# GLU chunk behind four gate chunks, S5 steps one per chunk, parameter rows on the sync queue, masks built late

## The reference

```
h      = rms_norm(x)
proj   = h @ w_in                 # q,k,v (512 each), u (256), q_mem (256), 3 x 1024 gate logits
o_na   = neighbourhood_attention(q, k, v, bias table)      # 8 heads, clamped 8 x 16 windows
o_s5   = GLU(gelu(bidirectional S5 state space layer(u)))   # 16 groups x 16 channels, 64 complex states
o_xa   = cross_attention(q_mem, rms_norm(mem) @ w_mem_kv)   # 4 heads, 256 memory tokens
merged = sum over the 3 branches of sigmoid(gate logits + b_gate) * (o_branch @ w_branch)
x      = x + merged @ w_out
x      = x + MoE(rms_norm(x))     # 16 experts of width 256 in 4 groups, top 2 in the best group
return rms_norm(x) * final_norm
```

## Time and profile before

| | us |
|---|---|
| median of 3 runs | 766.08 (764.28 to 766.26) |
| the profiled execution, its own time | 761.52 |
| its span | 759.9 |
| TensorE busy with matmuls | 648.5 (85%) |
| VectorE, ScalarE, GpSimd busy | 428.0, 325.2, 177.7 |
| mean granted TensorE clock | 0.933 of full |

### The profile page before, as it was taken

How to read it: one execution, slowest core, us unless ns; L and a number is a source line. 1 busy time by engine, 2 the same in 40 slices (tenths; PEclk the granted TensorE clock), 3 DMA queues, 4 the chain that set the end, 5 groups by cost and what they waited for, 6 DMA issues and landing times.

```text
span 759.9 us, 9239 instructions
## 1 busy us (share of the span) xinstructions
PE 648.5 (85%) x3201; PEld 512.7 (67%) x3201; DVE 428.0 (56%) x784; ACT 325.2 (43%) x549; POOL 177.7 (23%) x188
## 2 busy tenths in 40 slices
PE   1889899799799999999999997998378999989820
PEld 1667778697577776677777785887356777777610
DVE  5987016905623454334552259442667998999803
ACT  3872322203244333344322337222256787768612
POOL 7519819500000000000000000001363352324220
PEclk9999899989799999999999999998589999999965
DMA  9963112214121112411122224416968999999455
GB/s 287 183 157 104 36 40 72 84 56 111 30 81 56 56 56 76 146 57 56 55 70 70 83 84 136 146 56 244 351 199 294 324 383 363 354 345 319 114 80 225
DMA packets 88625, 114.73 MB, mean 151 GB/s; under 512 B 18336, under 2 KB 65538, under 8 KB 88584
## 3 DMA queue, kind: packets, MB, share of 16 engines
q1 hardware_dynamic: 74288, 92.56, 36.8%
q0 software_dynamic: 6848, 18.36, 10.0%
q10 hardware_dynamic: 7448, 3.27, 1.5%
HBM read 102.08 MB, written 15.80 MB: 155 GB/s over the span
## 4 chain that ended last, share of the span: by engine, by line
PE 55%; DMA 19%; DVE 11%; issue 6%; ACT 5%; POOL 2%; ACTq 1%; DVEq 0%; POOLq 0%; SPq 0%
DMA acc_scratch<-ysb,idx 17%; PE bank L1391 13%; PE bank L1393 12%; PE bank L1392 12%; PE bank L1571 3%; PE bank L1543 2%; PE bank L1560 2%; DVE w_lo L897 2%; PE bank L1547 1%; PE bank L1505 1%; PE bank L1481 1%; ACT w_hi L513 1%; POOL tok_scratch L1950 1%; DVE h_lo L922 1%; PE bank L1473 1%
## 5 line engine op out<-in xcount | busy, mean ns | idle before, releaser
L897 DVE TENSOR_TENSOR w_lo<-raw,w_hi 128x1024 fp32r<-128x1024 f32 x55 | 69.5, 1265 | 155.0 <-ACT w_hi L513 154.6
L1391 PE MATMUL bank<-h_hi,w_hi 128*128 128x512 f32 x320 | 131.8, 412 | 3.8 <-DVE w_lo L897 1.9
L1393 PE MATMUL bank<-h_hi,w_lo 128*128 128x512 f32 x320 | 125.3, 392 | 0.0
L1392 PE MATMUL bank<-h_lo,w_hi 128*128 128x512 f32 x320 | 125.0, 390 | 0.0
L1312 DVE TENSOR_TENSOR e_lo<-eraw,e_hi 128x2048 fp32r<-128x2048 f32 x48 | 108.5, 2286 | 12.8 <-ACT e_hi L796 12.8
L796 ACT CAST e_hi<-eraw 128x2048 fp32r<-128x2048 f32 x48 | 91.8, 1916 | 5.8 <-PE bank L1393 5.8
L1922 POOL DMA_DIRECT2D h_scratch<-h x4 | 2.2, 555 | 378.9 <-DVE h L1243 378.9
L1391 PEld LDWEIGHTS bank<-h_hi,w_hi 128*128 128x128 f32 x320 | 60.2, 188 | 18.6 <-DVE w_lo L897 2.6
L513 ACT CAST w_hi<-raw 128x1024 fp32r<-128x1024 f32 x55 | 57.4, 1044 | 34.5 <-PE bank L1393 34.5
L1393 PEld LDWEIGHTS bank<-h_hi,w_lo 128*128 128x128 f32 x320 | 60.0, 188 | 13.4
L1392 PEld LDWEIGHTS bank<-h_lo,w_hi 128*128 128x128 f32 x320 | 60.3, 189 | 10.5
(11 more groups left out here) (372 smaller groups left out, 1325.7 us busy)
## 6 DMA issues: line engine op xcount, KB each, us to landing
raw<-in_w_in SPq DMA_DIRECT2D x40, 512.0 KB, 3.8
eraw<-in_moe_w_gate SPq DMA_DIRECT2D x32, 512.0 KB, 7.3
eraw<-in_moe_w_up SPq DMA_DIRECT2D x32, 512.0 KB, 11.5
eraw<-in_moe_w_down SPq DMA_DIRECT2D x32, 512.0 KB, 9.4
raw<-in_w_out SPq DMA_DIRECT2D x8, 512.0 KB, 3.8
x_sb<-in_x SPq DMA_DIRECT2D x4, 512.0 KB, 5.2
raw<-in_w_mem_kv SPq DMA_DIRECT2D x4, 512.0 KB, 7.8
x_sb<-in_x SPq DMA_DIRECT2D x1, 2048.0 KB, 10.8
```

Source lines behind the costliest of these rows:

```text
L897: dve.tensor_tensor(v(l_, o, [1, 1024]), v(raw, 1024 * (c % RAW), [1, 1024]), raw32(v(h_, o, [1, 1024])), SUB).then_inc(sem("w_lo_done"), 1)
L1391: pe.matmul(dst, w[0], x[0], start=first, stop=False)
L1392: pe.matmul(dst, w[0], x[1], start=False, stop=False)
L1393: return pe.matmul(dst, w[1], x[0], start=False, stop=last)
```

## The change

- `C_GLU` goes from 20 to 24: four S5 gate chunks (20 to 23) now stand ahead of the GLU chunk, and the other four behind it. For that, `gt` lies in the room of x (42.5 KB) and no longer shares room with the split y, and the first gate's take has no wait for the GLU. The slots keep their places relative to the gate chunks. The first gate chunk waits until y has been taken out of banks 2 and 3.
- `s5_matrices` is cut in pieces: `turn_b` behind chunks 8 and 9 (16 transposes each, banks 4, 5, 7, 3), `lags` behind 10, `shifts` behind 11. `s5_inputs` goes from behind chunk 9 to behind 12. VectorE's steps go from 9 to 14 to 12 to 17, `s5_outputs` from behind 15 to behind 18, `gelu_arg` and `gelu` from steps 18 and 19 to 21 and 22. The rotations share one small buffer `turned_z`. The wait for the second turned memory value goes from the transposes to `shifts`.
- The bias flips are cut in two, two behind chunk 4 and two behind chunk 5, with ScalarE's copies.
- The eight parameter transfers go from ScalarE's queue to SyncE's, between the loads of chunks 0 and 1. The 16 transfers that bring y back go from ScalarE's to SyncE's, behind the load of chunk 25, with the wait for y in DRAM. The second load of x goes from between chunks 40 and 41 to behind all loads and the wait for the last product, ahead of the first expert weights.
- The ten mask instructions go on GpSimd from its start to behind the matrices `ca`.

The core of the diff:

```diff
-C_U, C_QX, C_MEMK, C_MEMV, C_Q, C_K, C_V, C_GLU = 0, 2, 4, 6, 8, 12, 16, 20
-C_S5G, C_S5P, C_XAG, C_XAP, C_NAG, C_NAP, C_OUT = 21, 29, 31, 39, 41, 49, 53
+C_U, C_QX, C_MEMK, C_MEMV, C_Q, C_K, C_V = 0, 2, 4, 6, 8, 12, 16
+C_S5G, C_GLU, C_S5P, C_XAG, C_XAP, C_NAG, C_NAP, C_OUT = 20, 24, 29, 31, 39, 41, 49, 53
...
-    gt = at("gt", R0 + 16, KD * SEQ)
+    gt = at("gt", 42.5, KD * SEQ)
...
         load(0)
+
+        def rows(w, r, n):
+            sp.dma_start(v(prm, 0, [1, P], p0=r, pn=n), w).then_inc(sem("prm_in"), 16)
...
-        for c in range(5, C_NAG):
+        for c in range(5, NCH):
             load(c)
-
-        sp.wait_ge(sem("s5_y"), 2)
-        sp.dma_start(v(x_sb, 0, [D, NT], [1, D]), x_nat).then_inc(sem("x_again"), 16)
-        for c in range(C_NAG, NCH):
-            load(c)
+            if c == 25:
+                sp.wait_ge(sem("y_out"), 16)
+                for g in range(G5):
+                    sp.dma_start(v(yT, SEQ * (g // 8), [K5, T5], [1, K5], p0=16 * (g % 8), pn=16),
+                                 y_dram.rearrange("(t c) (g k) -> c t g k", c=16, k=K5)[:, :, g, :]).then_inc(
+                                     sem("y_in"), 16)
...
         sp.wait_ge(sem("prod"), 24)
+        sp.dma_start(v(x_sb, 0, [D, NT], [1, D]), x_nat).then_inc(sem("x_again"), 16)
         load_unit(0, 0, 0)
...
-                elif m == 0:
-                    act.wait_ge(sem("s5_lo"), 2)
...
-            if c == 8:
-                take_s5_matrices()
-            if c == 15:
+            if c in (8, 9):
+                take_b(4 * (c - 8))
+            if c == 10:
+                take_lags()
+            if c == 11:
+                take_shifts()
+            if c == 18:
                 take_y()
-            if c == 16:
-                load_y()
-            if c == 18:
+            if c == 22:
                 act.wait_ge(sem("gelu_in"), 1)
...
-            if c in (9, 11):
-                rotate_in((c - 9) // 2)
-            if c in (10, 12):
-                scans((c - 10) // 2)
-            if c in (13, 14):
-                rotate_out(c - 13)
-            if c == 18:
+            if c in (12, 14):
+                rotate_in((c - 12) // 2)
+            if c in (13, 15):
+                scans((c - 13) // 2)
+            if c in (16, 17):
+                rotate_out(c - 16)
+            if c == 21:
                 gelu_arg()
-            if c == 19:
+            if c == 22:
                 gelu()
...
             if c == C_S5G:
+                pe.wait_ge(sem("y_took"), 1)
+            if c == C_S5G + 2:
                 pe.wait_ge(sem("v_took"), 6)
...
-            if c == 8:
-                pe.wait_ge(sem("bias_ready"), 4)
-                s5_matrices()
-            if c == 9:
+            if c in (8, 9):
+                turn_b(4 * (c - 8))
+            if c == 10:
+                lags()
+            if c == 11:
+                shifts()
+            if c == 12:
                 s5_inputs()
-            if c == 15:
+            if c == 18:
                 s5_outputs()
```

More of the change, by code:

```diff
@@ L66, in tiles_of @@
         return [("k", c - C_K)]
[L67 removed]
+    if c < C_S5G:
         return [("v", c - C_V)]
@@ L73, in tiles_of @@
             turns = TURNS.get(c, ())
-            return [(name + "t", j) for j in turns] + [(name + "g", c - first)]
+            return [(name + "t", j) for j in turns] + [(name + "g", c - first - (C_GLU < c < C_S5P))]
         if proj <= c < proj + 8 // per:
@@ L280, in chunk_src @@
         g0 = 3 * NAW + S5W + XAW
-        for first, branch in ((C_S5G, 1), (C_XAG, 2), (C_NAG, 0)):
-            if first <= c < first + 8:
-                return cols(w_in, g0 + D * branch + P * (c - first))
+        for first, last, branch in ((C_S5G, C_S5P, 1), (C_XAG, C_XAP, 2), (C_NAG, C_NAP, 0)):
+            if first <= c < last:
+                return cols(w_in, g0 + D * branch + P * (c - first - (C_GLU < c < C_S5P)))
         if C_S5P <= c < C_XAG:
@@ L729, in _ @@
                     turn_hi(b)
-            if c == C_MEMK:
-                for q in range(4):
+            if c in (C_MEMK, C_MEMK + 1):
+                for q in range(2 * (c - C_MEMK), 2 * (c - C_MEMK) + 2):
                     act.wait_ge(sem("flipped"), q + 1)
@@ L1037, in rotate_in @@
             z = [pv(zbank(d, r), 0, [K5, 8], [1, K5]) for r in range(2)]
-            t = [v(tmp, HALF * r + DW * d, [K5, 8], [1, K5]) for r in range(2)]
+            t = [v(turned_z, DW * r, [K5, 8], [1, K5]) for r in range(2)]
             dve.tensor_tensor(z[0], w[0], ph_of(d, 0), MUL)
@@ L1057, in rotate_out @@
             z = [pv(zbank(d, r), 0, [K5, 8], [1, K5]) for r in range(2)]
-            t = [v(wz, HALF * r + DW * d, [K5, 8], [1, K5]) for r in range(2)]
+            t = [v(turned_z, DW * r, [K5, 8], [1, K5]) for r in range(2)]
             dve.tensor_tensor(t[0], z[1], ph_of(d, 1), MUL)
@@ L1456, in product, with turn_b @@
             ins.then_inc(sem("tile"), 1)
-        def s5_matrices():
-            pe.wait_ge(sem("v_took"), 2)
-            pe.wait_ge(sem("ba_ready"), 1)
-            pe.wait_ge(sem("ba_back"), 1)
-            for q in range(8):
+        def turn_b(q0):
+            if q0 == 0:
+                pe.wait_ge(sem("bias_ready"), 4)
+                pe.wait_ge(sem("ba_ready"), 1)
+                pe.wait_ge(sem("ba_back"), 1)
+            for q in range(q0, q0 + 4):
                 if q >= 4:
@@ L1917, in _ @@
         pool.sem_inc(sem("ca_ready"), 1)
+        for kind, p0, pn in ((0, 64, 64), (1, 0, P), (2, 0, 64)):
+            mask(kind, p0, pn, 8, -1, 7)
+            mask(kind, p0, pn, -8, 1, 120)
+        for kind, p0, pn in ((0, 0, 64), (2, 64, 64)):
+            mask(kind, p0, pn, 8, 0, -64)
+            mask(kind, p0, pn, -8, 0, 184)
+        pool.sem_inc(sem("masks"), 1)
         for n in range(NT):
```

66 lines of the change are left out of this document (26 added, 40 removed).

## The result

The changed kernel takes a median of **745.97 us** (744.61 to 747.41, 4 runs), the kernel before 766.17 us (764.28 to 770.24, 4 runs). The ratio is 0.973 (95% interval 0.9685 to 0.9775). The forecast was 745.4. The profiled execution took 745.01 us, 16.5 us less than that of before; its span is 743.3 us.

What follows compares the result with a forecast made beforehand. TensorE was busy for 85% of the span, with winnable time in stages where it idles or its clock is down. Terms 3.0 + 1.7 + 7.9 + 0 + 8.1 = 20.7 us off the 766.08 median gave 745.4 us, range 737 to 756.

Steps and rivals of the forecast that it cites:

- Start: Kernel start: earlier ScalarE 0.8 us, masks moved off VectorE's work 2.5, less late rows; gain 3.0 us (0.5 to 4.5).
- 0 to 0.5 for the sum: Start: deduction in us for parameter rows landing late behind 2.5 MB in SyncE's queue; 2.5 at the high end.
- Bias flips: Flips behind chunks 4 and 5: only VectorE's idle 1.70 us is won, other gaps move; gain 1.7 us (0 to 3).
- S5 matrices: S5 matrix stage: gaps and low clock go, less 1.0 us for a fall at the lags; gain 7.9 (3.7 to 8.9).
- Rotations and outputs: S5 rotations and outputs: TensorE's wait stays near 3.5 us with the clock's fall; gain 0 us (-3 to +3).
- GLU: GLU chunk: four gate chunks hide y's path, 9.7 us won less 1.6 for GELU work; gain 8.1 (2 to 9.7).
- Second load of x: Second x load, issued where the expert weights went: lands in time, costed at nothing (0 to 4 us late).
- late parameter rows: Rival at the start: VectorE stands until rows land, all start gain lost, 748.4 us; a variant within the forecast's 0.60.
- three times more: Clock rival, chance 0.10: three more clock falls than counted, each costing 2.6 us, giving 753.2 us.
- stalled: Rival, chance 0.10: GELU work stalls slots fully (7.8 us, not 1.6), masks slow rotations by 3.0; 754.6 us.
- More is won: Rival, chance 0.11: states' wait shrinks (+3), start gives 4.5 (+1.5), flips 3 (+1.3); 739.6 us.
- the gaps only move: Rival, chance 0.04: TensorE's wait reappears in gate chunks, all but start and clock given back; 764 us.

## Why the prediction was right, point by point

The forecast of 20.7 us stands against 18.9 at the first product of `w_out`, 16.6 in the spans and 20.2 between the medians. That the median came out within 0.6 us is in part luck. The terms' errors are +2.1 us at the outputs and the GLU and -3.9 elsewhere, and the kernel before happened to be profiled 4.6 us below its median and the changed kernel 1.0: against the profiled execution the prediction gives 740.8, and 745.01 was measured.

- **Start, 3.0 forecast, 2.2 measured.** The masks were priced about right: 2.5 taken, 2.17 when they are put back, 3.15, just over the bound of 2.95, with the rows left on ScalarE's queue (19.97 to 16.82). The sign of the other part was wrong. Moving the rows was counted as +0.8 less 0 to 0.5; it measured -0.9 (-0.2 to -1.3 with the spread of the table), since VectorE's wait for `log_dt` (1.74) outweighs ScalarE's earlier start. The step that was off is "0 to 0.5 for the sum": the row was there at 12.1 us, not at the 10 to 10.8 that x's rate had given. The sum asked when the data ahead of the row would land; what made it late in the runs is that SyncE issues it only at 7.43 us. The rule cited from the Trainium skill (DMA: Bandwidth & Descriptors, Queues, rings and completion order) gave the right direction and size: a gain 0.5 to 1 us less. The trace agrees in the size, with 0.8 less than forecast. It does not show the reason, since the row took as long from its issue with the chunk ahead of it (4.7 us) as without (5.2).
- **Bias flips, 1.7 forecast, 0.45 measured**, and -1.3 to +0.6 with the spread: no gain that can be told. Right: the gap would turn into gaps at chunks 6 to 8. Missed: `forward_b` stands ahead of the split for chunk 7 (57.18 to 60.97), which ScalarE had made ready at 56.5, and the split then takes 1.98 us beside GpSimd. Ordering it the other way gives 3.7 us at this place.
- **S5 matrices, 7.9 forecast, 6.05 measured.** The 3.04 us gap was rightly priced, and the fall within the lags was foreseen, at 1.0 us; it lasted 6.75 us at half speed, about 3.4. These 2.4 more, less the 0.7 by which the inputs wait less for u (1.21 before, 0.52 now), are the missing 1.85 within 0.2. In the five other kernels with this code the gain is 2.4 to 5.6 us. But the reason was half wrong: "dealt out, the transposes wait for nothing" is due to the moved wait (3.00 us of gap when put back), not to the dealing out, which gives 0.4 us. The forecast that the clock stays above 0.95 from chunk 8 to 12 failed.
- **Rotations and outputs, 0 forecast, 1.65 measured.** The wait was forecast near 3.5 and is 3.62. GpSimd's masks (151.73 to 160.10) did not slow the rotations: the operations of the last one take 0.67 to 0.70 us, as in the kernel before. The gain is the clock, 3.5 us low in place of 7.0, and it is luck: in eight of the nine other kernels with this code the clock is low for 6.75 us again and the stretch gains 0.25 to 0.75. The forecast of 0 was the better reading.
- **GLU, 8.1 forecast, 8.5 measured.** Right, and it repeats within 0.1 us: no wait for the split y, small waits at exponentials (0.37). The margin is thin: y is split 1.5 us before its use, and two gate chunks less cost 5.9 us.
- **Second load of x, 0 forecast.** It landed 10.5 us after its issue and nothing waited for it. The first addition to x lies 18.1 us behind the first product of `w_out` (465.8 and 447.66) as against 17.35 before; the clock was low there for 7.0 us (453.25 to 460.25) and 3.25 before (474.25 to 477.5).
- **The rest.** From the first product of `w_out` to the end the profiled executions take 295.6 us (743.3 - 447.66) and 293.4 us before. Over the profiles of the eleven experiments this stretch, whose code none of them changes, takes 293.4 to 295.8. So the 2.3 us lost there are not told from the spread of this stretch, and were not traced further.

Of the rivals, the late parameter rows came true in that VectorE waits for them, and not at their full price: 0.2 to 1.3 us and not all 3.0 of the start. The clock fell three times up to the last gate of S5, where it had fallen five times, and not three times more; the slots waited 0.37 us, so they were not stalled. "More is won" was in reach only by edits that the change doesn't have. In "the gaps only move" 764 does not follow from its words: with the start's 3.0 us kept it would be 763.1 at most. SyncE's hold for y cost nothing: no product waited for a weight chunk there.

## What to carry to other kernels

Price a moved step by which wait it moves past, and undo the wait and the move apart: here one semaphore wait carried 3 us, and the dealing out around it 0.4. Read what one and the same stretch of code takes in several kernels before a difference of 1 to 4 us between two traces is given a cause: here the clock alone moved such stretches by up to 3 us. Small edits may not show in the total alone, and show together with others. A transfer moved off a busy engine's queue has to be placed by when it is wanted: behind one 512 KB load SyncE issued the last of eight small rows at 7.4 us, and it came 1.7 us late.

## What the runs showed of the hardware

- The granted clock fell from 1.0 to 0.5 with TensorE busy without a break, inside or behind the 8.25 us of lag products, in the eleven experiments too; in the changed kernel the 27.20 us of this stage have no idle time at a mean clock of 0.87. The low stretches there lasted 3.25 to 3.5, 6.75 to 7, or 10.25 us, and in one kernel 13.5. The three kernels with 6.75, 13.5 and 10.25 us (changed, rows on ScalarE's queue, `ba` one chunk later) have the same lag products, which begin at 88.99, 87.88 and 85.30 us.
- A low clock can be free: in the changed kernel it was low from 64.25 to 67.75, and TensorE then waited 0.86 us for VectorE; in four kernels where it held there, the same wait was 2.35 to 2.37 us.
- VectorE's split of 128x1024 takes 1.23 us, and 1.98 beside GpSimd's products for `ba`; the scaling pair takes 1.41 alone and 1.80 to 2.17 beside the masks. The rotations, which read one operand from PSUM, take 0.67 to 0.70 us beside the masks and without them. The Trainium skill (GPSIMD Engine Reference, 1. Specifications) says that GpSimd shares its memory interfaces with VectorE, and names two cases of contention: instructions with two inputs in SBUF and those in a two-port mode. The split is of the first kind and the trace agrees. The scaling has one such tensor and is slowed all the same; whether it is of the second kind, no row here tells.
